# First decode pages, the copies of the probabilities and two RWKV products, moved between queues and engines

## What is computed

```python
proj = x_ext @ w_in                       # q, k, v, f | r, k, v and low-rank inputs
logits = q @ k.T * HEAD_DIM ** -0.5 + c_q - c_k
attn = softmax(logits) @ v                # prompt: causal; samples: cached pages and themselves
k_page = cache_k[l][page_table]           # 8 sequences x 32 pages, also cache_v, cache_logf
# RWKV-7, per head
w_log = -softplus(-(w0 + tanh(wl) @ w2)) - 0.5
a = sigmoid(a0 + al @ a2)
kk = normalise(k * k_k);  k = k * (1 + (a - 1) * k_a)
S = S * w + (S @ -kk) * (kk * a) + v * k  # step by step over the tokens
y = S @ r
h = x + concat(attn, (groupnorm(y) + bonus) * g) @ w_out
h = h + (silu(hn @ w_gate) * (hn @ w_up)) @ w_down
```

## Time and profile before

| | us |
|---|---|
| three runs | 1513.98, 1517.31, 1509.17 |
| their median | 1513.98 |
| the profiled execution | 1510.73 |
| its span, first to last instruction | 1509.0 |

### The profile page before, as it was taken

How to read it: one execution, slowest core, us unless ns; L and a number is a source line. 1 busy time by engine, 2 the same in 40 slices (tenths; PEclk the granted TensorE clock), 3 DMA queues, 4 the chain that set the end, 5 groups by cost and what they waited for, 6 DMA issues and landing times.

```text
span 1509.0 us, 27895 instructions
## 1 busy us (share of the span) xinstructions
PE 1402.4 (93%) x11595; PEld 953.3 (63%) x11595; DVE 438.2 (29%) x917; ACT 357.0 (24%) x713; POOL 110.0 (7%) x223
## 2 busy tenths in 40 slices
PE   5999999988799999999989779999999999999997
PEld 4755666655577777777755454477777777744442
DVE  5022355455844444444445241310000000000002
ACT  3010233245444343443433331100000000000011
POOL 6283000000000000001202010000000000000000
PEclk9999899998799999999989889999999999999998
DMA  5187011023898787878957897003111221150001
GB/s 206 57 189 205 7 57 35 1 75 110 284 312 277 229 292 247 294 255 266 272 191 261 315 314 245 1 13 100 56 56 56 89 79 56 56 195 0 0 0 63
DMA packets 123174, 219.32 MB, mean 145 GB/s; under 512 B 11451, under 2 KB 35078, under 8 KB 123046
## 3 DMA queue, kind: packets, MB, share of 16 engines
q1 hardware_dynamic: 115154, 193.64, 38.3%
q0 software_dynamic: 7824, 23.85, 5.9%
q10 hardware_dynamic: 68, 0.02, 0.0%
HBM read 203.06 MB, written 14.41 MB: 144 GB/s over the span
## 4 chain that ended last, share of the span: by engine, by line
PE 84%; DVE 5%; DMA 4%; ACT 3%; issue 2%; SPq 1%; POOL 0%; DVEq 0%; POOLq 0%; ACTq 0%
PE PS L1369 23%; PE PS L736 13%; PE PS L1388 10%; PE PS L1178 6%; PE PS L1192 4%; PE PS L1308 4%; PE PS L1237 4%; PE PS L709 2%; DMA arena<-in_cache_k 2%; DMA out_wkv_prompt<-arena 1%; PE PS L1394 1%; PE PS L992 1%; PE PS L1002 1%; PE PS L996 1%; ACT arena L1622 1%
## 5 line engine op out<-in xcount | busy, mean ns | idle before, releaser
L1369 PE MATMUL PS<-arena 128*128 128x288 f32 x1408 | 342.1, 405 | 1.2 <-DVE arena L2251 1.2
L1369 PEld LDWEIGHTS PS<-arena 128*128 128x128 f32 x1408 | 265.7, 189 | 77.4 <-DVE arena L2251 1.4
L736 PE MATMUL PS<-arena 128*128 128x301 f32 (+1 forms) x736 | 197.7, 426 | 0.0
L1622 ACT ACTIVATE arena<-PS 128x512 f32<-128x512 f32 x256 | 141.4, 596 | 192.8 <-PE PS L1178 192.4
L1178 PE MATMUL PS<-arena 128*128 128x128 f32 x1024 | 153.8, 296 | 27.1 <-DMA arena<-in_cache_k 15.1
L736 PEld LDWEIGHTS PS<-arena 128*128 128x128 f32 (+1 forms) x736 | 136.6, 189 | 54.7 <-issue 13.6
L1178 PEld LDWEIGHTS PS<-arena 128*128 128x128 f32 x1024 | 122.1, 151 | 55.8 <-issue 24.2
L1388 PE MATMUL PS<-arena 128*128 128x512 f32 x352 | 151.5, 592 | 1.5 <-DVE arena L2277 1.5
L1388 PEld LDWEIGHTS PS<-arena 128*128 128x128 f32 x352 | 66.5, 189 | 86.2 <-issue 84.3
L2277 DVE TENSOR_TENSOR arena<-PS,arena 128x576 f32<-128x576 f32 x22 | 16.7, 758 | 327.0 <-ACT arena L1686 327.0
L1686 ACT ACTIVATE arena<-PS 128x576 f32<-128x576 f32 x22 | 14.3, 651 | 329.8 <-PE PS L1369 329.8
(11 more groups left out here) (360 smaller groups left out, 1409.9 us busy)
## 6 DMA issues: line engine op xcount, KB each, us to landing
arena<-in_cache_k SPq DMA_DIRECT2D x256, 256.0 KB, 4.3
arena<-in_cache_v SPq DMA_DIRECT2D x256, 256.0 KB, 4.8
arena<-in_w_gate SPq DMA_DIRECT2D x11, 1024.0 KB
arena<-in_w_up SPq DMA_DIRECT2D x11, 1024.0 KB
arena<-in_w_in SPq DMA_DIRECT2D x5, 2048.0 KB, 11.9
forgets_after<-arena POOLq DMA_DIRECT2D x64, 128.0 KB, 8.5
arena<-forgets_after SPq DMA_DIRECT2D x32, 256.0 KB, 5.1
arena<-in_w_down SPq DMA_DIRECT2D x4, 2048.0 KB
```

The lines of the kernel that those rows point to most:

```text
L736: ins = mm(PS[0:width, bank, 0:HALF], wring[:, c % 2, k, c0:c0 + width], xnT[:, k, half * HALF:(half + 1) * HALF], start=(k == 0), stop=(k ...
L1369: ins = mm(PS[:, 4 * (f % 2) + 2 * w + half, 0:HO], fring[r % FR][:, c:c + P], hT[:, k, half * HO:(half + 1) * HO], start=(k == 0), stop=( ...
L1622: av(KTs[:, (2 * i + q) % LOT], PS[:, T_USE[("k", L, i, q)] % 2, :].rearrange("p (g n) -> p g n", g=NG), ACT.Copy)\
```

## The change

- SP loads bias 0 and the first three key pages as soon as VectorE has taken the maximum of attention unit 24 (a new release of 6 in the loop, at u = 22); the fourth page waits for `v_free`, that is for attention's end. All counts of `k_free` fall by 2. The four value pages of lot 0 are issued before the keys of lot 1, no longer among them.
- TensorE turns page 0 of lot 0 before the scores of the new tokens; ScalarE copies it before their exponential.
- `take_probs` moves from VectorE to ScalarE, in the same piece.
- The two products of Bd move from VectorE to POOL, behind `hs_taken` of 4, a new count `rate_read` and `decays` of 3; VectorE waits for them (`ab_ready`) before the product that overwrites Kd. `N_PRE` falls from 17 to 15, and with it `N_RWKV` to 138.

```diff
@@ planner
-        N_PRE = 17
+        N_PRE = 15
@@ SP
             def key_page(pr, j, numbers, i):
-                sp.wait_ge(S["k_free"], pr * (2 * NPG) + (2 * LOT * j + 2 * i + 2))
+                if j == 0 and isinstance(pr, int):
+                    sp.wait_ge(S["k_free"], 6)
+                    if i == 3:
+                        sp.wait_ge(S["v_free"], LOT)
+                else:
+                    sp.wait_ge(S["k_free"], pr * (2 * NPG) + (2 * LOT * j + 2 * i))
...
-            sp.wait_ge(S["k_free"], 2 * LOT)
+            sp.wait_ge(S["k_free"], 6)
             numbers = load_lot(0, 0, 0, None, None)
-            for j in range(1, NLOT):
+            for i in range(LOT):
+                value_page(0, 0, numbers, i)
+            numbers = load_lot(0, 1, 0, None, None)
+            for j in range(2, NLOT):
                 numbers = load_lot(0, j, 0, j - 1, numbers)
@@ POOL
             pool.dma_start(G2, t_in["g2"][0]).then_inc(S["g2_in"], 16)
+            pool.wait_ge(S["hs_taken"], 4)
+            pool.wait_ge(S["rate_read"], NG)
+            ch(g.tensor_tensor(Bd, Bd, kk, ALU.mult))
+            pool.wait_ge(S["decays"], 3)
+            g.tensor_tensor(Bd, Bd, Kd, ALU.mult).then_inc(S["ab_ready"], 1)
             pool.wait_ge(S["pre_done"], 1)
@@ TensorE
                 for L in range(LOTS):
-                    turn_keys(L, 0)
+                    if L:
+                        turn_keys(L, 0)
                     yield
...
+            turn_keys(0, 0)
             new_scores(0)
@@ ScalarE
+            def take_probs(L):
+                act.wait_ge(S["pr_turned"], L + 1)
+                av(PTs, PS[:, T_USE[("p", L)] % 2, :].rearrange("p (a n) -> p a n", a=LOT), ACT.Copy).then_inc(S["pr_taken"], 1)
...
                     take_keys(L, 1)
                     yield
+                    if L:
+                        take_probs(L - 1)
...
+            act.wait_ge(S["v_free"], LOT)
+            take_keys(0, 0)
             exp_new(0)
@@ VectorE
+                if u == 22:
+                    v.memset(small[:, 5:6], 0.0).then_inc(S["k_free"], 6)
...
-            v.memset(small[:, 5:6], 0.0).then_inc(S["k_free"], 2 * LOT)
...
-                ch(tt(Bd, Bd, kk, ALU.mult))
-                yield
...
-                ch(tt(Bd, Bd, Kd, ALU.mult))
-                yield
                 ch(tt(AR[:, 1], XR[:, 0:4], AR[:, 1], ALU.mult))
                 yield
                 ch.wait()
+                dve.wait_ge(S["ab_ready"], 1)
                 ch(tt(Kd, XR[:, 4:8], Kd, ALU.mult))
...
-                    if L:
-                        take_probs(L - 1)
```

More of the change, by code:

```diff
@@ L185, in build @@
         ncb_ready ncb_taken s_ready s_added mx_ready exp_done p_ready pt_ready pt_taken pv_ready o_taken out_done
-        qb_ready kts_ready act_c dve_c pool_c pt_zero shn_turned shn_ready
+        ab_ready kts_ready act_c dve_c pool_c pt_zero shn_turned shn_ready
         lr_in lr_act lr_ready lr_taken hs_in hs_ready hs_rows hs_taken pre_done L_ready decays root_in root_done
@@ L191, in build @@
         fs_taken fs_out yc_ready rwkv_done prev_tile
-        k_free v_free wo_in x2_in gu_ready down_used ln_in y_final
+        k_free v_free wo_in x2_in gu_ready rate_read ln_in y_final
         kt_taken sc_taken sc_page nm_ready exp_out pr_turned pr_taken ov_ready ov_taken new_ready nmn_ready expn_out
@@ L477, in _ @@
                 if r == 2:
-                    sp.wait_ge(S["k_free"], 2 * LOT * (1 + LOTS))
+                    sp.wait_ge(S["k_free"], 2 * LOT * (1 + LOTS) - 2)
                     sp.wait_ge(S["sc_taken"], LOTS)
@@ L905, in rwkv_pre @@
                 yield
-                for _ in range(6):
+                for _ in range(4):
                     yield
@@ L1522, in rwkv_pre @@
                 yield
-                for _ in range(7):
+                for _ in range(5):
                     yield
@@ L1618, in take_keys @@
                 for q in range(2):
-                    act.wait_ge(S["k_free"], 2 * LOT * (L + 1) + 2 * i + q + 1)
+                    act.wait_ge(S["k_free"], 2 * LOT * (L + 1) + 2 * i + q - 1)
                     if L or i >= 2:
@@ L1636, in all_lots @@
                     pr, j = L // NLOT, L % NLOT
-                    take_keys(L, 0)
+                    if L:
+                        take_keys(L, 0)
                     yield
@@ L1664, in _ @@
             exp_lot(LOTS - 1)
+            take_probs(LOTS - 1)
             def mean_of_squares(n, i, turn):
@@ L1776, in _ @@
                     ins = v.tensor_copy(QB[64 * hp:64 * hp + 64, :, g, c:c + 8], samp(qT[64 * hp:64 * hp + 64, g, :], 1))
-            ins.then_inc(S["qb_ready"], 1)
             v.memset(PTm, 0.0).then_inc(S["pt_zero"], 1)
@@ L1901, in rwkv_pre @@
                 for g in range(NG):
-                    ch(ts(T2[:, g], Bd[:, g], -1.0, pc("k_a", g), ALU.add, ALU.mult))
+                    ts(T2[:, g], Bd[:, g], -1.0, pc("k_a", g), ALU.add, ALU.mult).then_inc(S["rate_read"], 1)
                 yield
-                ch.wait()
+                dve.wait_ge(S["rate_read"], NG)
                 ch(stt(XR[:, 4:8], T2, 1.0, XR[:, 4:8], ALU.add, ALU.mult))
@@ L2127, in add_sums @@
                 ch(tt(old, z, acc[:, L % 2:L % 2 + 1], ALU.add))
-            def take_probs(L):
-                dve.wait_ge(S["pr_turned"], L + 1)
-                v.tensor_copy(PTs, PS[:, T_USE[("p", L)] % 2, :].rearrange("p (a n) -> p a n", a=LOT)).then_inc(S["pr_taken"], 1)
             def take_new_probs(pr):
@@ L2255, in _ @@
             add_sums(LOTS - 1)
-            take_probs(LOTS - 1)
             add_residual(0)
```

## The result

The changed kernel takes 1530.62 us (median of 4 runs, 1523.01 to 1532.30) against 1511.76 of the kernel before beside it: a ratio of 1.0111, 95 % interval 1.0084 to 1.0139. It is slower by more than the 0.5 % that the prediction took for noise, and 10.6 us above the upper end of the forecast. The profiled execution took 1530.65 us, its span 1528.9; the span before was 1509.0, so this execution carries 19.9 us to explain.

A forecast was written before the change was run, and what follows sets the result against it. From 420 us on TensorE was its own bound (busy 389.3 of 420 us); from 329 to 420 it met waits and a lower clock. Terms +0.4 - 1.1 + 0 - 1.1 + 0 = -1.8 us gave 1512.2 us, range 1504 to 1520.

The forecast's parts named there:

- Pace: Later decode: 138 steps over the same 236 pieces, so every later step sits a little elsewhere; 0 us (-3 to +3).
- eighth low-rank product: Before lot 2: slips from piece 12 to 13, some 1.5 us; lot 2 starts +0.4 us (bounds -0.8 and +1.7).
- The bonus wait: TensorE's 3.78 us wait for VectorE's bonus (until 407.68) does not go; 0 us (bounds -3.8 and +3.8).
- First key pages: Lot 0: earlier loads remove the 3.21 us page wait, T2 is next; -1.1 us (bounds -2.27 and 0).
- four waits in a row: TensorE's waits of 2.29, 3.21, 3.98 and 3.78 us between the end of prompt attention (329) and 420 us.
- Products on POOL: Bd's two products, 5.63 us each on POOL; the 1.20 wait at 391.59 goes: -1.1 us (bounds -1.2 and 0).
- The rival with the hold: POOL's products each hold VectorE's next about 5 us; TensorE waits 5.3 at the bonus: 1517.5 us, chance 0.22.
- Probabilities by ScalarE: 32 copies leave VectorE, each 0.09 us shorter over twelve waits: -1.1 us (-4.8 to +6.6).
- Values ahead of lot 1's keys: Eight 256 KB issues before lot 1's keys, cover some 25 us: nothing; 8 us if the cover were gone.

The follow-up runs named there:

- e5: The whole change with 17 preparation steps as before, empty steps where VectorE's two products of Bd stood; POOL still makes them: 1515.11 us, ratio 1.0007.
- e14: The whole change, 15 steps, with TensorE's bonus sums one step later and VectorE's decayed receptance and Kd behind lot 2's maxima: 1519.77 us, ratio 1.0065.
- e6: The kernel before with 15 steps of preparation and nothing else; VectorE keeps all eight products: 1531.69 us, ratio 1.0122.
- e9: The kernel before with the early loads and the probabilities by ScalarE, 17 steps, all products on VectorE: 1511.03 us, ratio 0.9996.
- e1: The whole change without POOL: both products of Bd back on VectorE in the neighbouring steps, still 15 steps: 1522.56 us, ratio 1.0072.
- e4: The kernel before with only the copy of the probabilities moved to ScalarE: 1505.96 us, ratio 0.9960.
- e7: The whole change plus four matmuls that nobody reads, on TensorE in lot 0's wait for T2: 1517.82 us, ratio 1.0028.
- e17: The whole change, 15 steps, with only the planner dealing the steps by the old rate: 1517.37 us, ratio 1.0041.

## Why the prediction was wrong

*Pace: the step that failed.* The prediction said that every later step "sits a little elsewhere" and took 0, within -3 and +3. Alone the count of 15 costs 12.2 thousandths, 18 us [15, 22]. The rates 139/236 and 137/236 were written down, but spent on one step, the eighth low-rank product. The same sum moves the bonus sums and tile 0 three pieces forward; the prediction even names tile 0 at piece 26 instead of 29, "with the work of the three pieces behind it instead of ahead", and puts no price on it. On a fixed order, work that slides from ahead of a wait to behind it, while the wait ends when it did, costs its whole length: 3.4 us here, beside the 2.00 at tile 0 and 0.6 for a lower clock (4.17 for the bonus sums, 3.57 before). The rest came later: the bound of 3 us was taken from the idle time of 420 to 840 us at a mean clock of 0.99, but in the same trace the samples' part from 760 on stood at 0.94, with 11.5 of 80 us idle, and there the new places lowered the clock again.

*The bonus wait.* "3.8 beside 3.78: 0" compared the same wait with itself at another place. It measured 7.04, inside the bounds (+3.8) but not by their reason: VectorE's adds came at 417.24, right behind lot 2's maxima as foretold; what was missing is that TensorE arrives three pieces earlier. For VectorE to pass ScalarE's exponential of lot 2 the prediction had put 1.4 more ahead of tile 0; VectorE stood 6.30 for it between the two pairs of adds, part of which it would have waited for the second bonus sums anyhow, and TensorE 2.01.

*First key pages.* Foretold: row sums near 337.97 behind T2, at the lower level. Measured: 338.24, at 2.36. The moment and the level were right; the size was not. The surcharge was priced on two instructions (2.07 us) and the bounds were -2.27 and 0. The level stayed at 0.50 to 354, with TensorE busy for 15.76 of 16 us, and lot 0 ended 8.7 late; behind the same wait e5 and e14 ended it only 1.5 and 1.8 late, and one trace can't tell whether the long stay belongs to the kernel or to this execution. The "four waits in a row" also pass over a fifth, 2.64 for the spreads at 357.88, behind which the level was low as well; it grew to 3.81. The loads alone cost 3.0 thousandths, 4.6 us [0.9, 8.3]. The bound above should have been a loss: in the kernel before the granted clock had stood at 0.50 from 382 to 394 us behind the wait of 3.98, for much longer than two instructions, though behind the wait of 3.21 the row sums at 340.24 ran at the upper level again (1.38).

*The eighth low-rank product.* Foretold: a wait of about 5.5 for lot 2's first page, at 382 to 383. The wait was 5.76, and 5.56 in e6, where the turn began at 382.98 as foretold. In the changed kernel all of it lies 10 us later, since the preparation in lot 0 was late (SP's biases at 385.97).

*Products on POOL.* 5.63 each foretold, 5.61 measured. The rival with the hold was right in its mechanism: neighbours at 8.15 and 8.55; that the scans of the earlier trace rows showed no stop did not hold for these products. The Trainium skill's rule (SBUF — State Buffer, "SBUF: two separate sides"), an exclusive lock for the length of an instruction between a GpSimd instruction that reads SBUF and a VectorE instruction with two operands in SBUF, is what these rows show. But its price, 5.3 us at the bonus, was not what happened: with 17 steps the bonus wait is 4.6 beside the hold and 3.4 without it (e5 and e9). A rival can have the right mechanism and still not be the cause: without POOL e1 loses 7.2 thousandths, and with it e5 loses nothing that can be measured.

*Probabilities by ScalarE.* -1.1 foretold (-4.8 to +6.6); alone they gave -4.0 thousandths, 6 us [2.3, 9.7]. The wait of 1.20 at 391.59 is gone as said. e4's execution came 3.8 us late into the stage; it is 1.4 behind the kernel before at lot 1, 1.2 at lot 23, and 3.0 ahead at lot 31. So it gained 2.4 early, and 4.2 late, where VectorE is busy with the samples. That the copy no longer queues behind RWKV's steps there would explain the late part better than cheaper copies do; this is argued, no run shows it.

*Values ahead of lot 1's keys.* Nothing foretold; no wait for lot 1's pages appears in after.

## What to carry to other kernels

When the number of steps in a hand-dealt order changes, list every step's old and new piece and look at each wait of the trace: whatever slides from ahead of it to behind it is paid in full if the wait ends when it did, however small the shift in rate looks. Taking instructions away from an engine and giving their slots back are two edits; here the slots were load-bearing, and the kernel with the slots left empty lost nothing that could be measured. And where a load comes earlier but another wait stands right behind it, most of the idle time has only moved, here to a place where it lowered TensorE's clock ahead of a long run of work.

## What the runs showed of the hardware

- TensorE stayed at the lower level (0.50) from 338 to 354 us while it was busy for 15.76 of the 16 us; in e7, without the wait ahead of it, the stretch stood at 0.91.
- Behind the same wait of 3.78 us the level was back within 4.1 us of the row sums' start in e17, 10.9 in e5, 17.1 in e9 and 17.2 in the changed kernel (the first instruction wholly at the upper level starts at 346.06, 348.44, 354.24 and 355.42). Why was not settled.
- A VectorE product of two 128x2560 operands that starts 0.15 us behind POOL's product takes 8.15 us instead of 2.82: it waits for POOL's whole instruction. Four of 128x640 took 8.55 instead of 3.27.
- POOL's product of 128x2560 took 5.61 us, twice VectorE's 2.82.
